# A hybrid mixer and mixture-of-experts layer in f32: attention products in quarters of the array, the router in four strips, and a new order of work per tile

## What is computed

```python
proj = rmsnorm(x) @ w_in                       # u 512, q 256, k 256, v 512, r 512, z 16 columns
pool = window_means(u) - u                     # trailing windows 2, 4, 8, 16; then a 128x128 product per group
b    = cumsum(log_sigmoid(z @ w_gate_up + b_gate) / 16)        # per chunk of 64 tokens, 4 heads x 64
q_i, k_i, k_dec = q * exp(b) / 8, k * exp(-b), k * exp(b_last - b)
scores = tril(q_i @ k_i.T)                     # per chunk and head: 64 x 64, contraction over 64
kv     = k_dec.T @ v                           # per chunk and head: 64 x 128, contraction over 64
S_next = exp(b_last) * S + kv
o      = scores @ v + q_i @ S                  # then RMSNorm per head, * silu(r)
h      = x + concat(pool, o) @ w_out
hn     = rmsnorm(h)
logits = hn @ w_router                         # 4 groups + 32 experts = 36 columns; top-1 group, top-2 experts
y      = rmsnorm(h + sum(gate * expert(hn)))   # 32 experts: down(silu(x @ gate) * (x @ up)), 512 wide
```

## Time and profile before

| | |
|---|---|
| median of three runs | 1128.63 us |
| profiled execution, its own time | 1130.37 us |
| its span in the profile | 1128.4 us |
| PE busy | 1041.3 us, 92% of the span |
| DVE, ACT, GpSimd busy | 38%, 21%, 10% |
| mean granted TensorE clock | 0.966 of full speed |
| one pass of the mixer's loop | 54.26 us, six passes |
| one expert in the steady part | 16.84 us |

### The profile page before, as it was taken

One profiled execution on the slowest core, in us unless ns is written; L12 is line 12 of the kernel. 1 busy time (PEld: TensorE's weight loads), 2 busy tenths in 40 slices (PEclk: granted clock), 3 DMA queues, 4 the chain that ended last, 5 costly groups with the idle time before them and its releaser, 6 DMA issues.

```text
span 1128.4 us, 31328 instructions
## 1 busy us (share of the span) xinstructions
PE 1041.3 (92%) x13842; PEld 853.4 (76%) x13842; DVE 424.4 (38%) x918; ACT 242.5 (21%) x506; POOL 107.2 (10%) x174
## 2 busy tenths in 40 slices
PE   5999999999999999983999999999999999999920
PEld 5878787878786868642879889888888888888810
DVE  1416261616162626333353233233233223223238
ACT  2334141323232232111111111111111111111114
POOL 0110101010101010100101101101101101101000
PEclk9999999999999999986999999999999999999965
DMA  8900000000000000076799999999999999999557
GB/s 277 384 2 38 0 37 0 37 0 37 16 21 37 0 37 1 38 299 218 254 397 367 406 404 402 413 408 396 409 402 398 411 405 396 412 397 395 238 198 304
DMA packets 50844, 262.08 MB, mean 232 GB/s; under 512 B 8205, under 2 KB 10701, under 8 KB 42618
## 3 DMA queue, kind: packets, MB, share of 16 engines
q1 hardware_dynamic: 41050, 234.05, 52.6%
q0 software_dynamic: 7168, 18.10, 4.7%
q10 hardware_dynamic: 2592, 9.44, 2.1%
HBM read 241.84 MB, written 26.80 MB: 238 GB/s over the span
## 4 chain that ended last, share of the span: by engine, by line
PE 84%; DVE 10%; DMA 2%; issue 2%; ACT 1%; SPq 0%; ACTq 0%; DVEq 0%; POOLq 0%; POOL 0%
PE bank L1363 31%; PE bank L1155 17%; PE bank L1264 11%; PE bank L1374 10%; PE bank L1380 5%; PE bank L1143 4%; DVE er L809 2%; PE bank L1233 2%; DVE arena L1121 1%; DVE arena L1119 1%; DVE arena L1127 1%; DMA arena<-in_w_in 1%; PE bank L1257 1%; DVE hnT L864 1%; PE bank L1251 1%
## 5 line engine op out<-in xcount | busy, mean ns | idle before, releaser
L1155 PEld LDWEIGHTS bank<-xnT,arena 128*128 128x128 f32 x1728 | 198.8, 194 | 11.2 <-issue 7.7
L1155 PE MATMUL bank<-xnT,arena 128*128 128x128 f32 x1728 | 200.0, 277 | 3.1 <-DMA arena<-in_w_in 3.1
L1363 PEld LDWEIGHTS bank<-xnT,arena 128*64 128x64 f32 x4096 | 170.9, 138 | 8.0 <-issue 8.0
L1363 PE MATMUL bank<-xnT,arena 128*64 128x96 f32 x4096 | 174.1, 247 | 1.4 <-issue 1.4
L1363 PEld LDWEIGHTS bank<-hnT,arena 128*64 128x64 f32 x4096 | 169.7, 137 | 7.4 <-issue 7.4
L1363 PE MATMUL bank<-hnT,arena 128*64 128x96 f32 x4096 | 172.8, 246 | 0.6 <-issue 0.6
L1003 DVE TENSOR_SCALAR mixT<-mixT 128x384 f32<-128x384 f32 x32 | 11.5, 360 | 324.3 <-ACT mixT L684 282.4
L1264 PE MATMUL bank<-arena,mixT 128*128 128x512 f32 x288 | 128.0, 603 | 2.9 <-DVE mixT L850 2.9
L1264 PEld LDWEIGHTS bank<-arena,mixT 128*128 128x128 f32 x288 | 55.1, 194 | 70.0 <-issue 66.3
L1374 PE MATMUL bank<-arena,osq 128*32 128x384 f32 x768 | 86.6, 488 | 0.5 <-issue 0.5
L1374 PE MATMUL bank<-arena,silu_r 128*32 128x384 f32 x768 | 85.8, 487 | 0.5 <-issue 0.5
(11 more groups left out here) (195 smaller groups left out, 1016.7 us busy)
## 6 DMA issues: line engine op xcount, KB each, us to landing
arena<-in_w_eg SPq DMA_DIRECT2D x32, 2048.0 KB
arena<-in_w_eu SPq DMA_DIRECT2D x32, 2048.0 KB
arena<-in_w_ed SPq DMA_DIRECT2D x32, 2048.0 KB, 14.4
hn_rows<-hs ACTq DMA_DIRECT2D x18, 512.0 KB, 3.4
arena<-pick_rows SPq DMA_DIRECT2D x16, 512.0 KB, 10.3
arena<-in_w_in SPq DMA_DIRECT2D x3, 2048.0 KB, 14.5
arena<-in_w_out SPq DMA_DIRECT2D x1, 4096.0 KB, 25.3
out_y_prompt<-arena SPq DMA_DIRECT2D x8, 512.0 KB, 3.6
```

Of the source, the lines that this page charges most:

```text
L1155: last = mm(out, w_in_sb[:, k, a:b], xnT[:, k, :], start=k == 0, stop=k == KD - 1)
L1363: last = mm(out[q * SW:(q + 1) * SW, n * BLOCK:(n + 1) * BLOCK], w[:, k, m * P + q * SW:m * P + (q + 1) * SW], rowsT[b][:, k, :], start=k ...
```

## The change

Six things change together.

1. Scores, `kv` and the state part of the outputs are computed in 64x64 quarters of the array: rows by head (or by chunk, for `kv`), columns by the output's 64 partitions. Scores and `kv` become 8 calls each instead of 4, the state part 16 instead of 4. Quarters of different row halves write different PSUM banks. `q_i` and `kz` lose their zeros, and DVE and ACT write each in one operation instead of two.
2. The router's 8 products of 128 stationary columns become 32 of 32 columns, in four column strips.
3. PSUM: scores in banks 5 and 4, outputs in 4 and 6, `kv` in 3 and 2. DVE masks the scores in four operations of 64x128 instead of one of 128x512, and updates a state in two operations of 128x128 instead of four of 64x128. ACT squares the outputs in two operations, and DVE scales them in two.
4. PE's order: `head_means` goes behind the first eighth of q and k; `proj_r` ahead of `project_out`; `pool_mix` ahead of `proj_v`; `turn_h` into `proj_v`; `router` between `kv` and the outputs; `ranks` and `mark` move to the next body (tile i-2).
5. New or moved waits on PE: `proj_qk_gate` now begins with a wait for `sA_ready` (bank 2 holds `kv` of the second chunk), which before stood ahead of `proj_v`; scores wait for `mixp_ready`; `turn_x` waits for `hnT_ready`.
6. DVE and ACT follow: the chain of `back_route` is at the very end of the DVE body, behind `front_state`; `back_rank`, `back_idx` and `back_weights` run in the next body; `back_h` goes behind `front_silu`; on ACT `x_scale` goes ahead of `front_r`, `pool` ahead of `back_h`.

```diff
+        sc_bank, o_bank, kv_bank = (bank[5], bank[4]), (bank[4], bank[6]), (bank[3], bank[2])
...
-        kz = kz_v[:, 0:2 * PAIRS * P].rearrange("p (c a n) -> p c a n", c=2, a=PAIRS)
+        kz = kz_v[:, 0:PAIRS * P]
...
+                wait_parted(dve, s["pe_scores"], i + 1, s["parted"])
                 for r in range(2):
...
+                    got = sc_bank[r][:, 0:PAIRS * CHUNK].rearrange("p (a n) -> p a n", a=PAIRS)
+                    for c in range(2):
+                        own = slice(c * CHUNK, (c + 1) * CHUNK)
+                        V.copy_predicated(sc[own, r::2, own], causal_i[own, own].unsqueeze(1).to_broadcast([CHUNK, PAIRS, CHUNK]),
+                                          got[own]).then_inc(s["sc_ready"], 1)
...
             def proj_qk_gate(i, first=False):
                 if first:
                     pe.wait_ge(s["w_qk_in"], 16)
+                else:
+                    pe.wait_ge(s["sA_ready"], i)
                 for m in range(2 * PAIRS):
                     last = features(bank[2][:, m * P:(m + 1) * P], Q0 + m * P, Q0 + (m + 1) * P)
                     if m == 0:
+                        if not first:
+                            head_means(i - 1)
...
-                for h in range(HEADS):
-                    last = mm(bank[5][:, h * P:(h + 1) * P], k_i[:, h // 2, :], q_i[:, h, :], start=True, stop=True)
+                wait_parted(pe, s["mixp_ready"], i + 1, s["parted"])
+                for p in range(PAIRS):
+                    for c in range(2):
+                        for r in range(2):
+                            last = mm(sc_bank[r][half(c), p * CHUNK:(p + 1) * CHUNK], k_i[half(r), p, half(c)], q_i[half(r), p, half(c)],
+                                      start=True, stop=True)
...
+                            last = mm(kv_bank[c][half(r), p * DV:(p + 1) * DV], kz[half(c), h * DK:(h + 1) * DK], v_sb[half(c), h * DV:(h + 1) * DV],
+                                      start=True, stop=True)
...
+                        for d in range(2):
+                            for r in range(2):
+                                last = mm(o_of(r)[half(d), p, half(c)], state[half(r), p, half(d)], q_i[half(r), p, half(c)],
+                                          start=False, stop=True, skip_group_check=True)
...
                 for k in range(KD):
-                    last = mm(bank[7][:, 0:NL], hnT[:, k, :], w_r_sb[:, k, :], start=k == 0, stop=k == KD - 1)
+                    for q in range(4):
+                        own = slice(q * TG, (q + 1) * TG)
+                        last = mm(bank[7][own, 0:NL], hnT[:, k, own], w_r_sb[:, k, :], start=k == 0, stop=k == KD - 1)
...
                 proj_z(i, first)
-                if not first:
-                    head_means(i - 1)
                 proj_qk_gate(i, first)
+                if ranking:
+                    ranks(i - 2)
                 proj_u(i, first)
...
+                if ranking:
+                    mark(i - 2)
+                proj_r(i, first)
                 if not first:
                     project_out(i - 1)
-                proj_r(i, first)
+                pool_mix(i)
+                proj_v(i, 0, 6, first)
                 if not first:
                     turn_h(i - 1)
...
+                proj_v(i, 6, KD)
...
+                scores(i)
+                chunk_products(i)
+                if not first:
+                    router(i - 1)
+                outputs(i, first)
```

More of the change, by code:

```diff
@@ L638, in body @@
                     back_o(i - 1)
-                front_gates(i, first, second)
+                if second:
+                    scale_w_out(2, KD - 1)
+                if not (first or second):
+                    back_router(i - 2)
+                front_gates(i, first)
                 if second:
@@ L652, in body @@
                     x_scale(front, i + 1)
+                front_r(i, first)
+                front_pool(i, first)
                 if not first:
-                    back_router(i - 1)
+                    back_h(i - 1, second)
+                    back.end()
                 front_end(i, first)
@@ L936, in body @@
                 front_gates(i, first)
-                if not first:
-                    back_h(i - 1)
-                else:
+                if ranking:
+                    rank.begin(i - 2)
+                    back_rank(i - 2, third)
+                front_decays(i, first)
+                if ranking:
+                    back_idx(i - 2)
+                    back_weights(i - 2)
+                if first:
                     dve.wait_ge(s["pe_hist_T"], 1)
@@ L981, in _ @@
             back_route(j)
+            rank.begin(j)
             back_rank(j)
@@ L1228, in gla, with chunk_products @@
                 last.then_inc(s["pe_scores"], 1)
+            def chunk_products(i):
                 pe.wait_ge(s["v_ready"], i + 1)
-                pe.wait_ge(s["kz_ready"], 2 * i + 2)
-                for c, out, signal in ((0, bank[3], s["pe_kvA"]), (1, bank[6], s["pe_kvB"])):
-                    for p in range(PAIRS):
-                        last = mm(out[:, 2 * p * DV:(2 * p + 2) * DV], kz[:, c, p, :], v_sb[:, 2 * p * DV:(2 * p + 2) * DV],
-                                  start=True, stop=True)
-                    last.then_inc(signal, 1)
@@ L1242, in gla, with outputs @@
+                last.then_inc(s["pe_kv"], 1)
+            def outputs(i, first=False):
+                pe.wait_ge(s["sc_ready"], 4 * i + 4)
+                for p in range(PAIRS):
+                    for r in range(2):
+                        h = 2 * p + r
+                        mm(o_of(r)[:, p, :], v_sb[:, h * DV:(h + 1) * DV], sc[:, h, :], start=p == 0, stop=False, skip_group_check=True)
                 if first:
-                    pe.wait_ge(s["setup_pool"], 4)
+                    pe.wait_ge(s["setup_pool"], 2)
@@ L1333, in _ @@
             head_means(j)
-            project_out(j)
+            project_out(j, last=True)
+            mark(j - 1)
             pe.wait_ge(s["u_kept"], 2)
+            pe.wait_ge(s["sA_ready"], TILES)
             for n in range(2):
```

214 lines of the change are left out of this document (105 added, 109 removed).

## The result

| | before | changed |
|---|---|---|
| median | 1128.60 us (4 runs) | 1103.87 us (4 runs, 1103.76 to 1103.94) |
| ratio, 95% interval | | 0.9776 [0.9759, 0.9793] |
| profiled execution, its span | 1130.37, 1128.4 | 1103.76, 1101.9 |
| mean granted TensorE clock | 0.966 | 0.966 |
| one pass of the mixer's loop | 54.26 us | 51.50 us |

The forecast was 1103 us with a range of 1097 to 1117.

The account below looks back on a forecast made before the run. PE was taken to bound the kernel, busy 377.22 of 379 us. Gains of 15.9 + 3.2 + 3.0 + 1.5 + 2.2 = 25.8 us off the profiled 1130.4, less 1.7 to the median, gave 1103 us, range 1097 to 1117.

Parts of the forecast that it names:

- Router, 0.75: Router in the loop: 16 rounds of four at 0.040 us plus 0.1 for change of shape, 0.75 instead of 1.71.
- wait for the masks, 0.15: Ahead of the outputs, PE waits 0 to 0.3 us for DVE's masks, taken as 0.15; the router covers the rest.
- records' rate: Rival for router and state part: no more than four records per 0.107 us in the long run; 1116 us, chance 0.12.
- Quarters 0.40, 0.55, 0.65: Scores, `kv` and state part: all four quarters run at once, taking 0.40, 0.55 and 0.65 us a pass.
- row halves take turns: Rival for scores, `kv` and state part: only column halves overlap, 0.65 us more a tile; 1109 us, chance 0.20.
- one after another: Rival for scores, `kv` and state part: quarters run singly with loads shown, 7.7 us a tile; 1154 us, chance 0.06.
- Wait for sA, 0.40: Ahead of q and k: DVE's `sA` update needs 0.97 us, `proj_z` covers 0.57; a new wait of 0.40 every pass.
- Wait of turn_h, 0.1: At `turn_h`: the norm of h on ACT just fits, wait 0 to 0.2 us, taken halfway as 0.1.
- Waits that go, 0.39: `head_means` no longer waits for ACT (0.1 us), nor `pool_mix` to `ranks` for DVE (0.29), each pass.
- The clock: Rival at each tile's end: short products and waits let PE's clock fall, 25 us comes back; 1128 us, chance 0.04.
- forecast gain 2.65: One loop pass: what took 5.53 + 0.39 us would take 3.25, waits included.
- Tiles: Gains outside a single pass: tile 0 1.5 us, tile 1 3.2, tiles 2 to 7 15.9, tile 8 3.0, tail 2.2.

Follow-up runs that it names:

- scores_first: `kv_bank7` with `turn_k` and scores ahead of `turn_x` on PE, masks and `sB` update ahead of `x_turned` on DVE; 1099.55 us.
- router_strips_old: The kernel before with the router's products in four column strips and nothing else; 1126.90 us, ratio 0.9989.
- scores_x4: The changed kernel with the scores computed four times over, same values in the same place; 1108.77 us, ratio to before 0.9822.
- kv_bank7: The changed kernel with the second chunk's `kv` in bank 7's free half, the `sA` wait moved ahead of `proj_r`; 1100.29 us, on repeat 1100.78.
- order_only: The changed kernel's new order with the old whole-array products, whole router and old place of the `sA` wait; 1126.72 us, ratio to before 0.9986.
- products_only: The changed kernel's products and PSUM places with PE, DVE and ACT in the order of before; 1120.49 us, ratio to before 0.9940.
- rows_outer: The changed kernel with all calls of one row half before the other in scores, `kv` and state part; 1105.77 us, ratio to before 0.9794.

## Why the prediction was right

The mechanism and its likeliest case held; point by point, for one pass:

- *Router, 0.75, and wait for the masks, 0.15.* Measured 0.82 together. `scores_first` shows the router alone at 0.70, and `router_strips_old` the same. In the trace of `scores_first` its 64 records start within 0.57 us, in rounds of 0.033 after the first, and the next product follows 0.13 later: the round was forecast at 0.040, the change of shape at 0.1. The masks themselves took 1.29 (306.33 to 307.62) where 1.1 was forecast.
- *The rule that spoke against it.* The Trainium skill ("TensorE: Matmul & The Clock Gate", Part 1) puts starts at 25 ns apart at least. 64 records in 0.70 us are 0.011 us apart on average, and the 64 of `scores_x4` 0.015. The trace disagrees with the rule for records that go to different parts of the array, and the rival "records' rate" (1116) falls with it. For records on the whole array the changed kernel's trace agrees: the two of `ranks`, with 32 columns each, and the one behind them start at 318.83, 318.86 and 318.88 us, two steps in 0.05 us.
- *Quarters 0.40, 0.55, 0.65.* With the wait for `kz` the scores took 0.58 (forecast 0.65); `kv` 0.60, state part 0.66. `scores_x4` shows that four run at once; "row halves take turns" (1109) and "one after another" (1154) fall.
- *Wait for sA, 0.40.* Measured 0.28 over the 0.57 of `proj_z`. DVE's update took 0.60 as forecast (half of 1.26); but the change of shape ahead of `proj_z` cost PE some 0.1 in which DVE was already at work. `kv_bank7` took the wait away and gained 0.28 a pass.
- *Wait of turn_h, 0.1.* None: 0.89 + 5.15 us passed from `pool_mix` to `turn_h`, and the norm was done.
- *Missed:* costs at places that I had left at nothing. The outputs from the scores took 1.08 in place of 0.89, and `turn_k` 0.32 in place of 0.22. 0.29 a pass, about what the waits were forecast too long: two errors that cancel. `turn_k` is a change of shape ahead of the scores. Of the outputs' 0.19, half stands at their end, ahead of the state part's quarters, and half between their first two starts; since `order_only`, where nothing changes shape there, has 0.08 of it too, that half isn't shown to be the change of shape.
- *Waits that go, 0.39.* They went in `order_only`, 0.29 and 0.10; its whole pass is 0.30 below before.
- *The clock.* 0.966 in both spans, 1.00 in the changed kernel from 109 to 460 us, and no product in the loop doubled in length. That rival (1128) falls.

Sum of a pass: forecast gain 2.65 (2.67 by its own terms), measured 54.27 - 51.50 = 2.77. Tiles: tile 0 ended 1.83 earlier (54.35 to 52.52, the start of the next `proj_z`; forecast 1.5). About 0.6 of this was there when r began and has nothing to do with the products, and `before` and `router_strips_old`, whose tile 0 is the same code, differ by 0.96 at this place, so no agreement can be read from it. The same distance of tile 1 went from 54.93 to 50.98 us, 3.95 against 3.2: the old pass there held a wait of 0.43 for ACT that I hadn't counted. Tiles 2 to 7 took 325.70 before and 308.89 after, 16.81 against 15.9. Tile 8, up to the last output projection, took 58.18 and 55.76, 2.42 against 3.0; of the 0.6 missing, 0.4 is `head_means`, which there waits 0.78 us for ACT's squares where it waited 0.40. Tail: from the last output projection to the first expert's transposes the timelines have 534.30 - 493.16 = 41.14 before and 506.90 - 468.15 = 38.75 after, 2.39 against 2.2. All together 27.4 us by the first expert, where the sum said 25.8. Of that the stretch behind it gave 0.9 back, with unchanged code, which I had put at nothing. The profiled execution fell by 26.6 us and the median by 24.7, because the profiled one of before was 1.7 above its median, as the forecast took off. That 1103 came within 1 us of 1103.87 is partly luck: the gain up to the experts was 1.6 larger than the sum said, and the unchanged stretch behind them took 0.9 of it back.

What the forecast didn't say: how much of the gain hangs on both halves of the change together. It named DVE's silu and routing chain only as covered in the new order. `products_only` and `router_strips_old` show that in the old order this chain, and not PE, set when `ranks` could start: PE already waited some 0.3 us a pass for it, and the whole 1.0 us that the strips took off the router came back as a longer wait there. What the quarters saved behind `ranks` met a second wait, 0.82 for the masks, and 0.77 a pass was left.

## What to carry to other kernels

Where PE is busy 99% of a loop, look how far behind it the next chain is: before, the wait of `ranks` for DVE, 0.3 us a pass, was all that showed of a bound that swallowed the router's whole 1.0 us. A product that needs half the rows or few columns is worth splitting over the array even in f32, if neighbouring calls go to different parts and the row halves to different PSUM banks (all runs here keep the banks apart; whether that is needed, none tests). And each faster product is cover that another engine loses, so put the short independent ones (here the router) where PE would wait. Keep the number of changes between whole and split array small.

## What the runs showed that I had not expected

- Records to different parts start far closer than whole-array ones: 64 in 0.70 us for 32 stationary and 36 streamed columns.
- Matmuls of one row half started ahead of four records of the other half that are written before them, in every tile of `rows_outer`. Two runs of 8 records in that order cost the same as when interleaved, to 0.02 us; two of 16 cost 0.25 us more.
- A change of shape costs 0.1 to 0.15 us in these rows (`turn_k` 0.32 for 0.22, the transposes of `scores_first` 1.02 for 0.87).
- From the first expert to the end the same code took between 589.9 and 593.6 us, so a few tenths of a per cent between two of these kernels are better read from passes than from medians.
